# Stick-breaking heads of the first layer: q and k feature-major, the second part beside the softmax units

## What is computed

```python
h = x @ w_in
c_q, c_kv, k_rope, sb_qkv = jnp.split(h, [Q_LORA, Q_LORA + KV_LORA, IN_A], axis=-1)
q = rms_norm(c_q, q_norm_g) @ w_uq        # 8 heads, 64 + 32 with rope
kv = rms_norm(c_kv, kv_norm_g) @ w_ukv    # 8 heads, k 64, v 64
o_a = softmax(where(allowed, q k^T * 96**-0.5, -inf)) v
# stick-breaking, per head, d = 64
z = q_b k_b^T * 64 ** -0.5
log_beta = log_sigmoid(z)
log_rem = where(past, log_sigmoid(-z), 0)
between = cumsum(log_rem, reverse) - log_rem
o_b = where(past, exp(log_beta + between), 0) v_b
mix = concatenate([o_a, o_b]) @ w_out
```

## Time and profile before

| | |
|---|---|
| median of 3 runs | 1924.68 us (1922.54 to 1925.34) |
| profiled execution | 1924.86 us, span of its instructions 1923.5 us |
| busy, share of the span | PE 91%, weight loads 81%, VectorE 67%, ACT 47%, POOL 14% |
| mean granted clock of PE | 0.959 of full speed |
| DMA | 317.45 MB, 165 GB/s over the span |
| load of `rows` on POOL's queue | 2560 KB |

### The profile page before, as it was taken

How to read it: one execution, slowest core, us unless ns; L and a number is a source line. 1 busy time by engine, 2 the same in 40 slices (tenths; PEclk the granted TensorE clock), 3 DMA queues, 4 the chain that set the end, 5 groups by cost and what they waited for, 6 DMA issues and landing times. The chain is left out here.

```text
span 1923.5 us, 31630 instructions
## 1 busy us (share of the span) xinstructions
PE 1756.4 (91%) x11200; PEld 1566.5 (81%) x11200; DVE 1287.6 (67%) x2255; ACT 905.4 (47%) x1565; POOL 273.0 (14%) x155
## 2 busy tenths in 40 slices
PE   7768999887897999778988998999999999999997
PEld 6646999677777998667777998999999998888885
DVE  4455656785677666766655899577786656666665
ACT  4553444345444443444634443677775444333332
POOL 0120200030112000212210789400000000000000
PEclk9978999998998999988988999999999999999999
DMA  7512556737554557434322554444444555555553
GB/s 269 208 44 88 181 179 217 260 127 255 172 171 138 181 186 268 147 125 139 124 66 97 167 165 143 162 137 139 143 143 146 186 186 181 187 191 189 186 185 120
DMA packets 85597, 317.45 MB, mean 165 GB/s; under 512 B 9536, under 2 KB 9808, under 8 KB 84864
## 3 DMA queue, kind: packets, MB, share of 16 engines
q1 hardware_dynamic: 76464, 278.43, 43.7%
q10 hardware_dynamic: 7776, 26.50, 3.9%
q0 software_dynamic: 1264, 11.25, 1.6%
HBM read 315.08 MB, written 1.05 MB: 164 GB/s over the span
## 5 line engine op out<-in xcount | busy, mean ns | idle before, releaser
L201 ACT ACTIVATE wh<-ring 128x1024 fp32r<-128x1024 f32 x529 | 559.9, 1060 | 801.6 <-PE bank L236 730.7
L203 DVE TENSOR_TENSOR wl<-ring,wh 128x1024 fp32r<-128x1024 f32 x477 | 603.6, 1269 | 485.6 <-ACT wh L201 485.2
L234 PE MATMUL bank<-xh,wh 128*128 128x256 f32 x2008 | 583.0, 290 | 22.6 <-POOL wl L203 7.3
L235 PE MATMUL bank<-xl,wh 128*128 128x256 f32 x2008 | 573.5, 286 | 0.0
L236 PE MATMUL bank<-xh,wl 128*128 128x256 f32 x2008 | 573.1, 285 | 0.0
L234 PEld LDWEIGHTS bank<-xh,wh 128*128 128x128 f32 x2008 | 390.4, 194 | 29.7 <-issue 11.2
L235 PEld LDWEIGHTS bank<-xl,wh 128*128 128x128 f32 x2008 | 390.8, 195 | 1.2
L236 PEld LDWEIGHTS bank<-xh,wl 128*128 128x128 f32 x2008 | 390.4, 194 | 0.0
L234 PE MATMUL bank<-wh,wa_high 128*128 128x512 f32 x512 | 203.2, 397 | 2.8 <-issue 2.1
L235 PE MATMUL bank<-wl,wa_high 128*128 128x512 f32 x512 | 202.4, 395 | 0.0
L236 PE MATMUL bank<-wh,wa_low 128*128 128x512 f32 x512 | 202.2, 395 | 0.0
(11 more groups left out here) (434 smaller groups left out, 2325.7 us busy)
## 6 DMA issues: line engine op xcount, KB each, us to landing
ring<-in_stream SPq DMA_DIRECT2D x529, 512.0 KB, 3.3
ada<-in_w_ada ACTq DMA_DIRECT2D x48, 512.0 KB, 4.2
rows<-in_rows POOLq DMA_DIRECT2D x2, 2560.0 KB, 11.6
con<-in_early POOLq DMA_DIRECT2D x1, 2078.0 KB, 11.1
x_feature_major<-in_x_fm ACTq DMA_DIRECT2D x4, 256.0 KB, 7.9
x<-in_x_tm POOLq DMA_DIRECT2D x1, 1024.0 KB, 9.4
weighted<-in_subkeys POOLq DMA_DIRECT2D x1, 1024.0 KB, 5.1
out<-weighted SPq DMA_DIRECT2D x2, 512.0 KB, 2.7
```

The source lines that it names most:

```text
L201: C.activation(wh[q % AHEAD][:, :], ring[slot][:, :], ACT.Copy).then_inc(s_high, 1)
L203: low.tensor_tensor(wl[q % AHEAD][:, :], ring[slot][:, :], wh[q % AHEAD][:, :], ALU.subtract).then_inc(s_low, 1)
L234: T.matmul(o, left[0], right[0], start=start, stop=False, skip_group_check=True)
L235: T.matmul(o, left[0], right[1], start=False, stop=False, skip_group_check=True)
```

## The change

The pieces of stick-breaking q and k are laid out for `feature_piece`, so that q and k come out feature-major (`sb_piece`), straight into `sqT` and `skT`; their token-major tiles and their turns are gone. The order of the pieces becomes: c, k_rope, q and k of the first four heads, the four up-projections, q and k of the last four heads, v. Between these pieces stand the first part of each stick-breaking head (`sb_first`: scores, Abs, Exp) and the turns of MLA q and k in halves of four heads. Both barriers of all engines are gone; one barrier without PE stays. The four Ln follow the last projection. `softmax_heads` is removed; the units go through `softmax_stream`, and its `fill` takes the second part of a stick-breaking head at a time, over three steps, with two banks for scores and one for values. `ada_step` runs in every step, behind the unit's own work. In `softmax_stream` the number of output banks becomes free, and in the last block a wait for a delivery moves from `opened` to it. POOL issues the load of `silu_c` behind the rotation of k_rope and that of `rows` behind those of q.

```diff
@@ mixer_a
+        def sb_piece(kind, m, b, free):
+            pe.wait(free)
+            y = feature_piece(bank[b][:, 0:S])
+            C.wait_ge(*y)
+            dst, scale = (sqT, DH ** -0.5) if kind == "q" else (skT, 1.0)
+            moved[kind, m] = act.did(C.activation(dst[:, m, :], bank[b][:, 0:S], ACT.Copy, scale=scale))
+        def sb_scores(h, b, stop):
+            rs = slice((h % 2) * DH, (h % 2) * DH + DH)
+            T.matmul(b[:, 0:S], skT[rs, h // 2, 0:P], sqT[rs, h // 2, :], start=True, stop=stop, skip_group_check=True)
+            return pe.did(T.matmul(b[:, S:384], skT[rs, h // 2, P:S], sqT[rs, h // 2, P:S], start=False, stop=stop,
+                                   skip_group_check=True))
+        def sb_first(h, b, free):
+            pe.wait(moved["q", h // 2], moved["k", h // 2], free)
+            zd = sb_scores(h, bank[b], True)
+            C.wait_ge(*zd)
+            absd[h] = act.did(C.activation(az[h % 2][:, :], bank[b][:, 0:384], ACT.Abs))
+            C.wait_ge(*absd[h])
+            ex[h] = act.did(C.activation(lz[:, h, :], az[h % 2][:, :], ACT.Exp, scale=-1.0))
...
+        sb_first(0, 5, moved["k", 1])
+        sb_piece("q", 2, 2, q_read)
+        sb_first(1, 1, qn)
+        sb_piece("k", 2, 6, q_read)
+        sb_first(2, 5, ex[0])
+        pe.wait(qr, qn)
+        q1 = pair_turn(qT[:, 0:4, :], [lambda t, h=h: qa[:, t, h, :] for h in range(0, 4)], [vn], [bank[7], bank[0]])
+        sb_piece("q", 3, 3, kn)
+        sb_first(3, 1, ex[1])
+        q2 = pair_turn(qT[:, 4:8, :], [lambda t, h=h: qa[:, t, h, :] for h in range(4, 8)], [q1], [bank[7], bank[0]])
+        sb_piece("k", 3, 4, kn)
+        sb_first(4, 5, ex[2])
+        pe.wait(kc, kn)
+        k1 = pair_turn(kT[:, 0:4, :], [lambda t, h=h: ka[:, t, h, :] for h in range(0, 4)], [q2], [bank[7], bank[0]])
+        sb_first(5, 1, ex[3])
+        pe.wait(moved["q", 2], moved["k", 2])
+        y = project((xh, xl), KD, [bank[2][:, :], bank[6][:, :]])
+        sb_first(6, 5, ex[4])
+        sb_first(7, 1, ex[5])
+        k2 = pair_turn(kT[:, 4:8, :], [lambda t, h=h: ka[:, t, h, :] for h in range(4, 8)], [k1], [bank[7], bank[0]])
+        C.wait_ge(*y)
+        for t, b in ((0, 2), (1, 6)):
+            sv_in = act.did(C.activation(sbv[:, t, :], bank[b][:, :], ACT.Copy))
+        for h0 in range(0, NH, 2):
+            act.wait(ex[h0 + 1])
+            ln = act.did(C.activation(lz[:, h0:h0 + 2, :], lz[:, h0:h0 + 2, :], ACT.Ln, bias=1.0))
+        release()
...
+        ada["every"] = 1
         act.wait(later["c"])
         ada["cond"] = act.did(C.activation(ada["silu_c"][:, :], ada["silu_c"][:, :], ACT.Silu))
...
+        def sb_softplus(h):
+            V.wait_ge(*scored[h])
+            dve.wait(ln)
+            s1 = dve.did(V.scalar_tensor_tensor(lz[:, h, :], zb[h % 2][:, 0:384], 0.0, lz[:, h, :], ALU.max, ALU.add))
+            V.wait_ge(*s1)
+            spz[h] = dve.did(V.tensor_tensor(lz[:, h, :], lz[:, h, :], cst("past_neg"), ALU.mult))
+        def sb_sums(h):
+            b = zb[h % 2]
+            T.wait_ge(*spz[h])
+            T.matmul(b[:, 0:384], cst("suffix"), lz[:, h, :], start=False, stop=False, skip_group_check=True)
+            cum[h] = pe.did(T.matmul(b[:, P:S], ones, lz[:, h, S:384], start=False, stop=True, skip_group_check=True))
+        def sb_left(h):
+            V.wait_ge(*cum[h])
+            dve.wait(weighed.get(h - 2))
+            left[h] = dve.did(V.scalar_tensor_tensor(az[h % 2][:, :], zb[h % 2][:, 0:384], 0.0, cst("past_add"),
+                                                     ALU.min, ALU.add))
+            C.wait_ge(*left[h])
+            act.wait(valued.get(h - 2))
+            weighed[h] = act.did(C.activation(wz[h % 2][:, :], az[h % 2][:, :], ACT.Exp))
+        def sb_values(h):
+            T.wait_ge(*weighed[h])
+            if h % 4 == 0:
+                pe.wait(operand["ready"][2 + h // 4 - 1] if h else sv_in)
+            valued[h] = pe.did(values_T(head_region(bank[7], h), wz[h % 2],
+                                        [sbv[:, s, h * DH:(h + 1) * DH] for s in range(2)]))
+            if h % 4 == 3:
+                deliver(2 + h // 4, bank[7], valued[h])
+        def fill(st):
+            ada_step()
+            if st < NH:
+                pe.wait(left.get(st - 2))
+                scored[st] = sb_scores(st, zb[st % 2], False)
+            if 0 <= st - 1 < NH:
+                sb_sums(st - 1)
+            if 0 <= st - 2 < NH:
+                sb_values(st - 2)
+            if st < NH:
+                sb_softplus(st)
+            if 0 <= st - 1 < NH:
+                sb_left(st - 1)
...
+        inner = softmax_stream(units, cst("chunked"), QKD ** -0.5, bank[0:2], bank[2:4], [bank[4]], mixed, give, masked, fill)
```

More of the change, by code:

```diff
@@ L452, in deliver @@
                                                       ALU.subtract))
[L454 to L533, removed]
-                b = bank[5 + h // 4 % 2]
-                pe.wait(moved[u])
-                if h % 4 == 0 and first and h >= 8:
-                    pe.wait(operand["ready"][base // 2 + h // 4 - 2])
-                valued[u] = pe.did(values_T(head_region(b, h), pt[u % 2], v, first and not opened_by, last_of_head))
-                if h % 4 == 3 and last_of_head:
-                    deliver(base // 2 + h // 4, b, valued[u])
-        release()
-        scope.close()
@@ L760, in mixer_a @@
-        sb_done = c
+        sb_piece("q", 0, 5, None)
+        sb_piece("k", 0, 6, None)
+        turned = []
+        pe.wait(*normed)
+        for j in range(2):
+            for kk in range(2):
+                for t in range(NT):
+                    k = 2 * j + kk
+                    last = T.transpose(bank[3 + j][:, kk * S + t * P:kk * S + (t + 1) * P], cn[:, t, k * P:(k + 1) * P], ident)
+            turned.append(pe.did(last))
+        for k in range(4):
+            dve.wait(turned[k // 2])
+            g = dve.did(V.tensor_scalar(cT[:, k, :], bank[3 + k // 2][:, (k % 2) * S:(k % 2 + 1) * S],
+                                        vcol("qkv_norm", k), None, ALU.mult))
@@ new lines, in mixer_a @@
+        later["rows"] = load_behind(12, rows[:, :, :], a["rows0"].unsqueeze(0).broadcast_to([P, 5, D]), "rows0")
+        y = project((ch[:, 2:4, :], cl[:, 2:4, :]), 2, bank[3:5])
+        C.wait_ge(*y)
+        for t in range(NT):
+            kn = act.did(C.activation(ka[:, t, :, 0:NOPE], bank[3 + t][:, :].rearrange("p (h d) -> p h d", h=NH), ACT.Copy))
+        pe.wait(moved["q", 1], qn)
+        y = project((ch[:, 2:4, :], cl[:, 2:4, :]), 2, [bank[7][:, :], bank[0][:, :]])
+        C.wait_ge(*y)
@@ L823, in mixer_a @@
-        for h in range(NH):
-            b = bank[h]
-            rs = slice((h % 2) * DH, (h % 2) * DH + DH)
-            T.matmul(b[:, 0:S], skT[rs, h // 2, 0:P], sqT[rs, h // 2, :], start=True, stop=False,
-                     skip_group_check=True)
-            zd = pe.did(T.matmul(b[:, S:384], skT[rs, h // 2, P:S], sqT[rs, h // 2, P:S], start=False,
-                                 stop=False, skip_group_check=True))
-            act.wait(zd)
-            ab = act.did(C.activation(az[:, h, :], b[:, 0:384], ACT.Abs))
-            act.wait(ab)
-            ex[h] = act.did(C.activation(lz[:, h, :], az[:, h, :], ACT.Exp, scale=-1.0))
@@ L2258, in layouts @@
     uq_rope = np.pad(uq[:, :, NOPE:].reshape(2, P, 256).transpose(1, 0, 2).reshape(1, P, HALF), ((0, 0), (0, 0), (0, HALF)))
+    stick = [between(eight_tiles(a_in[:, 544 + m * P:544 + (m + 1) * P]), eight_tiles(a_in[:, 1056 + m * P:1056 + (m + 1) * P]))
+             for m in range(4)]
     def ffn(l):
```

148 lines of the change are left out of this document (45 added, 103 removed).

## The result

| | before | changed |
|---|---|---|
| median of 4 runs each | 1924.94 us (1922.54 to 1925.34) | 1908.65 us (1905.18 to 1912.22) |
| span of the profiled execution | 1923.5 | 1903.8 |
| PE busy | 1756.4 (91%) | 1761.2 (93%) |
| mean granted clock of PE | 0.959 | 0.964 |

The ratio is 0.9916, 95% interval 0.9898 to 0.9934: 16.3 us faster. The profiled execution of the changed kernel was the fastest of its four.

A forecast was written before the change was run, and what follows sets the result against it. Chained waits in the first mixer bound the kernel. Projections ending at 83.7, first Exp at 97.3 and a 47.4 us stream start the output projection at 144.7 instead of 153.14, 8.4 us earlier: 1916.4 us, range 1909.5 to 1923.6.

The forecast's parts named there:

- What bounds the kernel: First mixer, 89.62 to 153.14 us: no engine full, engines wait in a chain, delaying the output projection.
- Part one: Projections with score pairs and turns moved in: last piece ends at 83.7 instead of 78.7 us, bounds 82 to 86.
- The 1 us that I put on ScalarE: In the projections: ScalarE waits at the late piece's split, the first turn's copies queue behind, delaying the second turn.
- The stall of 2.19 us: PE's wait at 62.86 us for a late piece; with the slow matmuls behind it 4.2 us, all forecast to go.
- The chain on ScalarE: ScalarE work between last piece and first softmax Exp: 13.6 us, so that Exp starts at 97.3 instead of 93.16.
- rival E: Every table load on ScalarE also costs a drain of about 1.38 us: 4.1 us more, 1920.5; chance 0.03.
- The stream: Merged softmax units and heads' second parts: 47.4 us from first Exp to last value against 60.0, at 5.0 a step.
- B: In the merged stream VectorE and PE hold each other: 6.2 us a step instead of 5.0, 1923.6; chance 0.13.
- D: Low PE clock stays through half of the stream: with five slow steps 16.0 us more, 1932.4; chance 0.07.
- C: Better case: ScalarE keeps up in the projections (82) and a stream step is PE's 4.5 us: 1911.2; chance 0.12.
- Five reductions earlier: nothing: Five more adaLN reductions in the first mixer and fewer later cost nothing; without cover, 1.15 us each.
- what follows is left as it is: Everything behind the output projection's start keeps its time; a move of more than 1 us would show the prediction wrong.

The follow-up runs named there:

- the second execution: The changed kernel run again with no edit: median of 6 runs 1910.42 us, ratio 0.992.
- the last experiment: Changed kernel with seven adaLN loads instead of eleven and Silu moved from before the first softmax Exp into the stream's second step: 1905.9 us, ratio 0.992.
- the shift: adaLN call count moved by one after the first mixer: kernel before with it 1926.68 us (ratio 1.0012); changed kernel with its old count restored 1910.31 us (0.9932).
- one half alone: Changed kernel with the stick-breaking heads' second parts run after all softmax units instead of beside them: 1932.44 us, ratio 1.0036.
- the other: Kernel before with its old projections, turns and barriers, then eight first parts and four Ln in a row, then the merged stream: 1922.69 us, ratio 0.9993.

## Where the prediction was right and where it failed

**What bounds the kernel** held: the mixer's chains of waits were the only place with much to win, and 13.1 of some 14 to 16 us came from there. I had forecast 8.4 for it. In the second execution the output projection started 4.6 us before the 144.7 of the forecast: 3.2 of them are the stream's, 0.6 those of ScalarE's chain and 0.8 those of part one.

**Part one** was forecast to end at 83.7. It ended at 80.8 in the profiled execution and 82.9 in the second; taking the start of each execution out (26.2 and 28.4 us for the first nine pieces, 28.8 before), that is 83.3 and 83.2. The 1 us that I put on ScalarE behind the late piece did not come: its split waited 2.98 us for the ring, up to 63.83, but all that stood behind it there, up to the copies of the turn, was done by 67.1, and PE came to its next turn at 67.76. PE did not stop. The stall of 2.19 us with its slow piece went entirely, as forecast. Of the two reasons that I gave for it, the later issue of `rows` can hardly be the one: it was issued at 50.10 before and at 51.05 now, and a piece still came late. That PE needs its pieces more slowly is left, but no run moves that load alone.

**The chain on ScalarE** was 13.0 us (80.8 to 93.77) against 13.6. Its members are all there with their durations; I had counted the four Ln at 3.3, they took 3.04 as a group. What I had called hidden, masking and maxima of the first units, is hidden only because Silu is there: the last experiment took it out and the wait appeared. The table loads at 85.76, 90.11 and 92.48 are each followed by their first activation after 1.29 us. The time by the rule on a drain (rival E) would have been 4.1 us longer; these rows, like the earlier trace rows, show none of it.

**The stream** is the term that failed, by its size: 47.4 us forecast, 44.4 and 44.2 measured. The step of 5.0 us in it was too long, as was the wait for the first adaLN tile. In the profiled execution the difference of 3.0 has three places. The first step cost 6.0 instead of 7.0: the tile was issued beside the first Exp, not a full 1.0 us behind it, so VectorE stood 1.62 us and not 3. The five steps between the third and the last masking took 28.8 instead of 30.4: full-clock steps were 4.85 and 4.5 where I had 5.0, the two with deliveries 6.6 and 6.4 where I had 7.1, the slow one 6.5 where I had 6.2. Last step and tail took 9.6 instead of 10.0. The clean step is 4.68 on the average. VectorE's sum of 4.98 for it was too high: I had three passes over 384 columns at their listed 0.55, 1.65 together, and in a row they take 1.53 (98.25 to 99.78); and every second step is 0.5 shorter, as I had said and not used. PE's sum of 4.53 was too low: I took a score pair at 0.70, by the longer of its matmuls, and one of a single head takes 0.85 (107.31 to 108.15). With that PE's sum is 4.68, just what the steps took. So the allowance for handing over was not needed: the two engines are as good as equal, and PE runs without a gap. A delivery cost 1.7 to 1.9 over the 4.7 of the steps without one, not 2.1.

**Rivals.** B (6.2 per step) fell: only the steps at low clock or with a delivery were that long. D (low clock through half of the stream) fell too: it lasted to 105.8 us, one step beyond the gap, and came back for 3.4 us at the second delivery, which I had not foreseen. But my reason against D was wrong. I had said that the clock rises when PE is busy without a break; with Silu in the stream it stayed low through 16 us of just that. The experiment with the second parts behind the units shows that its mechanism is real in this kernel and was close: once the two parts don't fill each other's gaps, the clock is between 0.50 and 0.85 in every stretch of 10 us and the change is a loss. C was the nearest in time, 1911.2 against measured 1908.65 and 1910.42, and partly by luck: its steps of PE's length came, its early end of part one (82) did not, and it has no term for the second layer.

**"Five reductions earlier: nothing"** and **"what follows is left as it is"** were the other misses; the prediction itself had named a move of over 1 us behind the output projection as a sign of being wrong. Reductions are not free in the stream (8 us for ten), and how many remain decides what comes at 774 us. And the number of calls of `ada_step` was not preserved: pieces 97 to 120 became 5 us shorter, of which the shift shows 4. Why the loads cost less beside the other pieces stays open. I had read the code of that counter and not counted its calls.

## What to carry to other kernels

Two chains that each leave an engine half idle can be worth much more interleaved than their busy times suggest, where the gaps also hold the clock down: here 22 us, 15 of them gaps and 7 slower work, against the 6 to 8 that I had expected. But such a change is worth its money only whole: one half alone was 7 us slower than the kernel before (ratio 1.0036), the other no different from it. When a loop with a shared counter is replaced, count its calls: what hangs on the counter moves everywhere behind it.

## What the runs showed of the hardware

- A reduction over 128 x 1024 float32 on VectorE took 1.22 us alone. Four took 2.69 to 3.40 us beside a multiplication or addition of two 128 x 1024 tensors on POOL (3.20 to 3.32 us each), and each of them ended 1.08 to 1.09 us behind the end of POOL's instruction (777.77 and 778.86; 781.11 and 782.19). The one that began 0.25 us before POOL's first took 1.22 us (774.30 and 774.55). That looks like waiting for POOL's instruction to end rather than like slower work. The Trainium skill (VectorE: DVE Perf Modes, Two Vector instructions with no wait between them) names a second read interface of VectorE that GpSimd shares, which a reduction of two SBUF tensors would need; the rows agree with that, and no run here tests it alone. The seven late reductions took 16.4 us together where seven times 1.22 are 8.5, and VectorE stood for their tiles 0.64 and 2.17 us besides.
- How long PE took to come back to full clock did not follow from its gaps. Counted from the end of the last piece, the clock was up after 14.9 us without reductions, 24.0 with six, 25.0 and 24.7 with ten, and 21.3 with six and Silu in the stream. Between the first scores and that moment PE had stood, at the most, for 0.27, 1.85, 2.5, 2.4 and 0.27 us at a time: the first and the last do not differ in this, and in the last it took 6 us longer. What decides it stays open.
- Spare matmuls of 512 columns in a row did raise the granted clock to 1.00 in all of 95 to 142.55 us, and the way from the last piece to the output projection still became 4 us longer (61.4 against 57.2).
